# Second attention of a two-block network on TensorE: where the turned meta columns go, when the small block is turned, and a new order of work at the end of a layer

## The reference

```python
proj = h @ w_in[l]                       # 2048 x 5120
c_val, c_glu, c_gate, q, k, v, a_gate, r_x, r_gate = split(proj)
c = conv31(c_val * sigmoid(c_glu)); c = silu(layer_norm(c)); c = c @ conv_pw_w + conv_pw_b
y_conv = c * silu(c_gate)
att = window_attention(rotary(q), rotary(k), v, sinks)   # 16 heads of 64; 16 meta keys, window, sink column
y_attn = att * silu(a_gate)
r = conv4(r_x); r = rg_lru(r)            # two gates (sigmoid), exp, sqrt, scan over positions
y_lru = r * silu(r_gate)
h = layer_norm(ALPHA * h + concat(y_conv, y_attn, y_lru) @ w_out[l])
```

## Time and profile before

| | |
|---|---|
| median of 3 runs | 2809.16 us (2803.56, 2809.16, 2809.18) |
| profiled execution | 2803.59 us, its span 2801.7 us |
| TensorE products / weight loads | 2730.8 us (97%) / 2440.9 us (87%) |
| VectorE / ScalarE / GpSimd | 1828.4 us (65%) / 1416.5 us (51%) / 142.8 us (5%) |
| mean granted TensorE clock | 0.99 |

### The profile page before, as it was taken

One profiled execution on the slowest core, in us unless ns is written; L12 is line 12 of the kernel. 1 busy time (PEld: TensorE's weight loads), 2 busy tenths in 40 slices (PEclk: granted clock), 3 DMA queues, 4 the chain that ended last, 5 costly groups with the idle time before them and its releaser, 6 DMA issues.

```text
span 2801.7 us, 45189 instructions
## 1 busy us (share of the span) xinstructions
PE 2730.8 (97%) x16993; PEld 2440.9 (87%) x16993; DVE 1828.4 (65%) x2402; ACT 1416.5 (51%) x2188; POOL 142.8 (5%) x138
## 2 busy tenths in 40 slices
PE   8999999999999999999999999999999999999897
PEld 7888888888888888888888888888998899998786
DVE  7566565656565666666566656657888676788665
ACT  6444444444454544444444445445745754645764
POOL 0000000000000010101001010000000000000000
PEclk9999999999999999999999999999999999999998
DMA  6555555555555555655555555555543345543353
GB/s 212 183 180 180 180 180 179 180 178 182 180 181 187 180 166 177 186 177 180 178 179 182 177 180 180 181 185 182 171 136 121 113 157 170 163 143 117 118 173 120
DMA packets 472884, 474.43 MB, mean 169 GB/s; under 512 B 17832, under 2 KB 468032, under 8 KB 472512
## 3 DMA queue, kind: packets, MB, share of 16 engines
q1 hardware_dynamic: 472528, 472.93, 54.1%
q10 hardware_dynamic: 256, 0.11, 0.0%
HBM read 470.86 MB, written 2.13 MB: 169 GB/s over the span
## 4 chain that ended last, share of the span: by engine, by line
PE 89%; DVE 6%; ACT 4%; issue 1%; DMA 0%; SPq 0%; ACTq 0%; DVEq 0%
PE proj L1226 34%; PE proj L1228 17%; PE proj L1241 9%; PE proj L1412 5%; PE proj L1413 5%; PE proj L1414 5%; PE proj L1243 4%; PE proj L1653 2%; DVE scratch L2209 1%; DVE w_both L2040 1%; PE proj L1655 1%; PE ps_s L1313 1%; PE ps_s L1296 1%; PE ps_t L1303 1%; ACT w_both L871 1%
## 5 line engine op out<-in xcount | busy, mean ns | idle before, releaser
L1226 PE MATMUL proj<-operand,w_both 128*128 128x512 f32 x4096 | 1451.6, 399 | 5.5 <-ACT x_res L698 5.4
L1715 DVE TENSOR_TENSOR w_both<-w_raw,w_both 128x1024 fp32r<-128x1024 f32 x644 | 807.3, 1256 | 693.3 <-ACT w_both L662 692.4
L662 ACT ACTIVATE w_both<-w_raw 128x1024 fp32r<-128x1024 f32 x644 | 681.9, 1059 | 922.2 <-PE proj L1228 708.7
L1228 PE MATMUL proj<-operand,w_both 128*128 128x256 f32 x4096 | 1144.7, 279 | 0.0
L1226 PEld LDWEIGHTS proj<-operand,w_both 128*128 128x128 f32 x4096 | 769.7, 188 | 186.4 <-issue 6.2
L1228 PEld LDWEIGHTS proj<-operand,w_both 128*128 128x128 f32 x4096 | 773.1, 189 | 0.8
L1412 PE MATMUL proj<-operand,w_both 128*128 128x272 f32 (+1 forms) x1540 | 456.8, 297 | 4.5 <-DVE operand L2276 4.5
L1413 PE MATMUL proj<-operand,w_both 128*128 128x272 f32 (+1 forms) x1540 | 448.9, 292 | 0.0
L1414 PE MATMUL proj<-operand,w_both 128*128 128x272 f32 (+1 forms) x1540 | 447.9, 291 | 0.0
L2040 DVE TENSOR_TENSOR w_both<-w_raw,w_both 128x1024 fp32r<-128x1024 f32 x226 | 277.7, 1234 | 174.8 <-ACT w_both L871 173.7
L1241 PE MATMUL proj<-w_both,operand 128*128 128x512 f32 x1024 | 363.2, 399 | 0.0
(11 more groups left out here) (347 smaller groups left out, 2052.9 us busy)
## 6 DMA issues: line engine op xcount, KB each, us to landing
w_raw<-in_a_w_in_dram SPq DMA_DIRECT2D x256, 512.0 KB, 3.7
w_raw<-in_w_in_dram SPq DMA_DIRECT2D x160, 512.0 KB, 3.6
w_raw<-in_b_w_in_dram SPq DMA_DIRECT2D x128, 512.0 KB, 3.8
w_raw<-in_kv_w_dram SPq DMA_DIRECT2D x128, 512.0 KB, 3.9
w_raw<-in_a_w_out_dram SPq DMA_DIRECT2D x64, 512.0 KB, 4.5
w_raw<-in_b_w_out_dram SPq DMA_DIRECT2D x64, 512.0 KB, 3.6
w_raw<-in_w_out_dram SPq DMA_DIRECT2D x64, 512.0 KB, 3.4
scratch<-in_a_rel_bias_dram SPq DMA_DIRECT2D x16, 256.0 KB, 3.7
```

The source lines that it names most:

```text
L662: act.activation(w_hi[:, s], w_raw[:, s], ACT.Copy).then_inc(hi_ready, 1)
L1226: pe.matmul(proj[:, 2 * bank + t, :], w_hi[:, s, kk, cols], rhs[:, k, :], start=first and k == 0, stop=False)
L1228: m = pe.matmul(proj[:, 2 * bank + t, 0:S], w_lo[:, s, kk, cols], rhs[:, k, 0:S], start=False, stop=last and end)
L1715: dve.tensor_tensor(w_lo[:, s], w_raw[:, s], w_hi[:, s].bitcast(F32), ALU.subtract).then_inc(pieces_split, 1)
```

## The change

- The two turned blocks of meta columns from `s2` go to the fourth quarter of `ps_t`'s two banks, beside the other turned columns. `turn_probabilities` no longer waits for `proj_free`.
- The small block (16 x 16, from `sm`) is turned by `turn_meta_probabilities` halfway through piece 1, still into the bank of the output made before, and still behind `proj_free`. `sm` gets a second buffer (`sms`).
- `copy_turned` copies the two blocks and the other columns. A new `copy_turned_meta` copies the small block and counts `ptm_ready`. It stands behind `exponentials(i)` and one `hi`, ahead of `copy_head_outputs(i-1)`.
- The squares of the convolution go to two buffers (`conv_squares`), and both square sums follow one another.
- `TAPS_DURING` for the pairs goes from 2, 3, 4, 4, 4, 4, 1, 0 to 3, 4, 3, 3, 3, 3, 3, 0, with up to two taps ahead of the reciprocals.
- The order of ScalarE's and VectorE's work at the end of the layer is dealt anew.

```diff
 def copy_turned(i):
     act.wait_ge(turned_2, PAIRS_2 * l + i + 1)
-    bank = (o0 + U_PAIR + i) % 2
-    act.activation(ptm[0:2 * META], proj[0:2 * META, 2 * bank, 0:T], ACT.Copy).then_inc(ptm_ready, 1)
+    act.activation(ptm[0:2 * META, META:T].rearrange("p (t n) -> p t n", t=2), ps_t[0:2 * META, :, 3 * P:4 * P], ACT.Copy)
     act.activation(pt2, ps_t[:, :, 0:384], ACT.Copy).then_inc(pt2_ready, 1)
+
+def copy_turned_meta(i):
+    act.wait_ge(small_turned, PAIRS_2 * l + i + 1)
+    act.activation(ptm[0:2 * META, 0:META], proj[0:2 * META, 2 * ((o0 + U_PAIR + i) % 2), 0:META], ACT.Copy)\
+       .then_inc(ptm_ready, 1)
...
 exponentials(i)
 hi(1)
 if i >= 1:
+    copy_turned_meta(i - 1)
     copy_head_outputs(i - 1)
 divide_by_sums(i)
...
 hi(1)
 copy_turned(7)
+copy_turned_meta(7)
...
+act.wait_ge(c_centred, l + 1)
 square_conv(0)
+square_conv(1)
 hi(1)
 act.wait_ge(y_ready, 4 * l + 1)
 hi_of(att[:, 0:4, :], slice(0, 4))
-hi(1)
 copy_head_outputs(7)
-square_conv(1)
-gate_tanhs(2, a_gates[:, 4:8, :])
-hi(1)
 act.wait_ge(lru_v_ready, l + 1)
 act.activation(lru_r, lru_r, ACT.Sqrt).then_inc(lru_root, 1)
-take(U_CGATE, c_gates[:, 0:2, :], 0.5)
 hi(1)
 act.wait_ge(c_mean_ready, l + 1)
 act.activation(c_rstd, c_mean, ACT.Sqrt).then_inc(c_root_ready, 1)
+hi(1)
+take(U_CGATE, c_gates[:, 0:2, :], 0.5)
+gate_tanhs(2, a_gates[:, 4:8, :])
 gate_tanhs(3, r_gates)
 hi(1)
-act.wait_ge(y_ready_pool, l + 1)
-hi_of(att[:, 4:8, :], slice(4, 8))
 hi(1)
 act.wait_ge(c_scaled, l + 1)
...
 gate_tanhs(4, conv)
+act.wait_ge(y_ready_pool, l + 1)
+hi_of(att[:, 4:8, :], slice(4, 8))
 hi(1)
 act.wait_ge(y_ready, 4 * l + 2)
 hi_of(lru_t, slice(8, 12))
+hi(1)
 take(U_CGATE + 1, c_gates[:, 2:4, :], 0.5)
-hi(1)
 act.wait_ge(gate_used, 5 * l + 4)
 hi_of(conv, slice(12, 16))
...
 # TensorE
-    pe.wait_ge(proj_free, o0 + output + 3)
...
-    out = proj[0:2 * META, 2 * bank, :]
-    pe.transpose(out[:, 0:META], sm[0:META, 0:META, :].rearrange("p c h -> p (c h)"), ident[0:META, 0:META])
-    pe.transpose(out[:, META:144], s2[:, 0:META, :].rearrange("p c h -> p (c h)"), ident)
-    m = pe.transpose(out[:, 144:T], s2[:, 146:162, :].rearrange("p c h -> p (c h)"), ident)
+    pe.transpose(ps_t[0:2 * META, 0, 3 * P:4 * P], s2[:, 0:META, :].rearrange("p c h -> p (c h)"), ident)
+    m = pe.transpose(ps_t[0:2 * META, 1, 3 * P:4 * P], s2[:, 146:162, :].rearrange("p c h -> p (c h)"), ident)
     m.then_inc(turned_2, 1)
+
+def turn_meta_probabilities(i):
+
+    output = U_PAIR + i
+    pe.wait_ge(proj_free, o0 + output + 3)
+    pe.transpose(proj[0:2 * META, 2 * ((o0 + output) % 2), 0:META],
+                 sms[i % 2][0:META, 0:META, :].rearrange("p c h -> p (c h)"), ident[0:META, 0:META]).then_inc(small_turned, 1)
...
 turn_probabilities(i - 1)
 score(i)
-pieces(unit, norm, (1,))
+pieces(unit, norm, (1,), halfway=lambda: turn_meta_probabilities(i - 1))
 head_values(i - 1)
...
 # VectorE, layer's end
 dve.scalar_tensor_tensor(lru_r, lru_r, 1.0, lru_t, ALU.add, ALU.mult).then_inc(lru_v_ready, 1)
 lo(1)
-y_lo_of(2, att[:, 0:4, :], slice(0, 4))
-silu_of(2, a_gates[:, 4:8, :], a_gates[:, 4:8, :])
-lo(1)
 dve.wait_ge(c_sq_summed, 2 * l + 2)
 dve.tensor_scalar(c_mean, ps_s[:, 1, 0:T], 1.0 / CONV_D, LN_EPS, ALU.mult, ALU.add).then_inc(c_mean_ready, 1)
+y_lo_of(2, att[:, 0:4, :], slice(0, 4))
 dve.wait_ge(lru_root, l + 1)
 dve.wait_ge(lru_ix, l + 1)
 step(dve.tensor_tensor(lru_r, lru_r, lru_i, ALU.mult))
+lo(1)
 for t in range(CT):
     m = dve.tensor_tensor_scan(lru_t[:, t, :], lru_a[:, t, :], lru_r[:, t, :], 0.0, ALU.mult, ALU.add)
-lo(1)
 step(m)
+lo(1)
 dve.wait_ge(c_root_ready, l + 1)
 step(dve.reciprocal(c_rstd, c_rstd))
 step(refine(c_rstd, c_mean, conv_sq[:, 0, :]))
-lo(1)
 dve.tensor_tensor(conv, conv, over(c_rstd, CT), ALU.mult).then_inc(c_scaled, 1)
+silu_of(2, a_gates[:, 4:8, :], a_gates[:, 4:8, :])
+lo(1)
 silu_of(3, r_gates, r_gates)
 lo(1)
+dve.tensor_tensor(lru_t, lru_t, r_gates, ALU.mult).then_inc(y_ready, 1)
+lo(1)
+silu_of(4, conv, conv)
 y_lo_of(3, att[:, 4:8, :], slice(4, 8))
-dve.tensor_tensor(lru_t, lru_t, r_gates, ALU.mult).then_inc(y_ready, 1)
-lo(1)
-silu_of(4, conv, conv)
 lo(1)
 y_lo_of(4, lru_t, slice(8, 12))
-lo(1)
-y_lo_of(5, conv, slice(12, 16))
 ...
+lo(1)
+y_lo_of(5, conv, slice(12, 16))
```

More of the change, by code:

```diff
@@ L274, in build_program @@
         pt2 = two.take(2, 384)
-        sm = two.take(META + 1, 2)
+        sm_even = two.take(META + 1, 2)
         turn_t = two.take(2, T)
@@ L299, in build_program @@
         conv_sq = two.take(2, T)
+        sms = [sm_even, two.take(META + 1, 2)]
+        conv_squares = [conv_sq, s2.rearrange("p c h -> p (c h)")[:, 0:2 * T].rearrange("p (a b) -> p a b", a=2)]
         chunk_sum, chunk_mean, chunk_m2, chunk_off = (two.take(2, OUT_N) for _ in range(4))
@@ L1014, in divide_by_sums @@
                 def divide_by_sums(i):
+                    sm = sms[i % 2]
                     act.wait_ge(recip_2_ready, PAIRS_2 * l + i + 1)
@@ L1104, in square_conv @@
                 def square_conv(half):
[L1105 to L1108, removed]
+                    act.activation(conv_squares[half], conv[:, 2 * half:2 * half + 2, :], ACT.Square).then_inc(c_squared, 1)
                 hi(1)
                 copy_turned(7)
+                copy_turned_meta(7)
                 act.wait_ge(conv_tap, TAPS * (l + 1))
@@ L1422, in next_split, with multiply_piece @@
                 return p % PIECES
-            def multiply_piece(banks, operand_2, chunk, first, last, width=T):
+            def multiply_piece(banks, operand_2, chunk, first, last, width=T, halfway=None):
                 s = next_split()
                 for kk in range(PK):
+                    if kk == PK // 2 and halfway is not None:
+                        halfway()
                     k = chunk * PK + kk
@@ L1435, in _, with pieces @@
                 raw, norm, y = raws[l], norms[l], ys[l]
-                def pieces(output, operand_2, chunks, width=T):
+                def pieces(output, operand_2, chunks, width=T, halfway=None):
                     bank = 2 * ((o0 + output) % 2)
@@ L1442, in pieces @@
                             pe.wait_ge(proj_free, o0 + output + 1)
-                        multiply_piece(proj[:, bank:bank + 2], operand_2, chunk, chunk == 0, chunk == PIECES - 1, width)
+                        multiply_piece(proj[:, bank:bank + 2], operand_2, chunk, chunk == 0, chunk == PIECES - 1, width, halfway)
                 def mean_sums():
@@ L1628, in conv_square_sums @@
                     for t in range(2):
-                        m = pe.matmul(ps_s[:, 1, 0:T], ones, conv_sq[:, t, :], start=half + t == 0, stop=half + t == 2)
+                        m = pe.matmul(ps_s[:, 1, 0:T], ones, conv_squares[half][:, t, :], start=half + t == 0, stop=half + t == 2)
                     m.then_inc(c_sq_summed, 1)
@@ L1633, in _ @@
                 turn_probabilities(7)
-                pieces(U_CGATE, norm, (1,))
+                pieces(U_CGATE, norm, (1,), halfway=lambda: turn_meta_probabilities(7))
                 head_values(7)
                 conv_square_sums(0)
-                pieces(U_CGATE, norm, (2,))
                 conv_square_sums(1)
-                pieces(U_CGATE, norm, (3,))
+                pieces(U_CGATE, norm, (2, 3))
                 pieces(U_CGATE + 1, norm, (0, 1, 2, 3))
@@ L2251, in score_maxima @@
                     by_head = s2.rearrange("p c h -> p h c")
-                    meta_by_head = sm[0:META].rearrange("p c h -> p h c")
+                    meta_by_head = sms[i % 2][0:META].rearrange("p c h -> p h c")
                     dve.tensor_tensor(by_head[:, :, 0:144], mask_2[:, 0:144].unsqueeze(1).to_broadcast([P, 2, 144]),
@@ L2329, in _ @@
                 step(refine(c_rstd, c_mean, conv_sq[:, 0, :]))
+                dve.tensor_tensor(conv, conv, over(c_rstd, CT), ALU.mult).then_inc(c_scaled, 1)
+                silu_of(2, a_gates[:, 4:8, :], a_gates[:, 4:8, :])
                 lo(1)
-                dve.tensor_tensor(conv, conv, over(c_rstd, CT), ALU.mult).then_inc(c_scaled, 1)
                 silu_of(3, r_gates, r_gates)
                 lo(1)
-                y_lo_of(3, att[:, 4:8, :], slice(4, 8))
                 dve.tensor_tensor(lru_t, lru_t, r_gates, ALU.mult).then_inc(y_ready, 1)
@@ L2337, in _ @@
                 silu_of(4, conv, conv)
+                y_lo_of(3, att[:, 4:8, :], slice(4, 8))
                 lo(1)
                 y_lo_of(4, lru_t, slice(8, 12))
-                lo(1)
-                y_lo_of(5, conv, slice(12, 16))
                 if l + 1 < DEPTH:
```

20 lines of the change are left out of this document (12 added, 8 removed).

## The result

The changed kernel takes 2861.49 us (median of 4 runs, 2856.81 to 2862.66), the kernel before 2808.97 us on the same chip (2803.56 to 2809.18): a ratio of 1.0188, 95% interval 1.0175 to 1.0200. It is slower by 52.5 us. The profiled execution took 2856.81 us, 53.2 more than the profiled one before; its span is 2855.0 us (2801.7 before). The mean granted clock of TensorE is 0.98.

A forecast was written before the change was run, and what follows sets the result against it. TensorE, carrying 89% of the chain, was taken as the bound, losing time in pauses and at its lower clock. Attention's 39.2 and the layer ends' 9.6 gave +49 us on 2803.6 or 2809.2: forecast 2855 us, range 2828 to 2882.

The forecast's parts named there:

- The wait that comes: At head_values, waiting for the new small copy: a new pause of 3.1 us in 14 of 16 pairs.
- T+10.65: Predicted start of head_values in pair 1, 10.65 us behind the turn's start T; that pair 22.9 us.
- The clock: TensorE behind each new pause: the lower clock costs 1.6 us a pause, bounds 0 and 3.4.
- clock stays up: Rival, chance 0.12: TensorE's clock does not drop in the new pauses; 22 us less, 2833 us.
- long drop: Rival, chance 0.11: turns do not count as clock-gate work like products, so drops near 6.98 us; +25, 2880 us.
- A pair's length: Attention: a usual pair takes 21.0 us; the stretch sums to 154.3 us, +20.0 and +19.2 in the two layers.
- The layer's end: Turn 8 to pointwise product: hand-overs make TensorE wait 11.7 us for y_lo_of(3); +5.7 us, in layer 2 +3.9.
- All 15.2 us go, and with them some 6 of the clock's loss: Ahead of the turn: the 8 pauses ending with an output's take-out vanish, 15.2 us, plus some 6 us of lower clock.
- Faster: Rival, chance 0.03: the small copy comes within 5.6 us of the turn, so head_values is not late; 2795 us.

The follow-up runs named there:

- edit 1: The changed kernel with the small copy issued right behind copy_turned, ahead of the exponentials, as the only edit: 2783.42 us, ratio 0.9930.
- edit 4: The changed kernel with 25 unused products of 224 columns ahead of head_values, keeping TensorE at work in the pause: 2834.80 us, ratio 1.0116.
- edit 8: Edit 1 with the convolution taps dealt over the pairs as before the change: 2813.51 us, ratio 1.0038.
- edit 9: The kernel before with only the new dealing of the taps, the turn keeping its blocks, banks and waits: 2786.29 us, ratio 0.9927.
- edit 3: The changed kernel with the layer's end (square sums, engine orders) as before the change: 2845.05 us, ratio 1.0150.
- edit 7: The changed kernel with y_lo_of(3) moved three steps earlier on VectorE, ahead of the recurrent product: 2857.67 us, ratio 1.0194.
- edit 6: Edit 1 with another order of ScalarE's and VectorE's work at the layer's end: 2761.79 us, ratio 0.9851.
- edit 10: Edit 6 with silu_of(2) two lo later, so GpSimd's product runs beside the reciprocal, and one hi moved: 2764.23 us, ratio 0.9840.

## Why the prediction was right, and the step that was not

The forecast was 2855 us with a range of 2828 to 2882, and 2861.5 was measured; on the profiled execution 2852 against 2856.8. By its own steps:

- **The wait that comes** was the right mechanism at the right place. head_values starts 8.60 us behind its turn (8.75 predicted) in pairs 2 to 6 and waits 2.93 us (3.1). Pair 1 was predicted at T+10.65 and came at 10.55, with a pause of 4.90 us. Edit 1 shows the cause, since moving only that copy takes all 14 pauses away.
- **The clock** was sized at 1.6 us a pause; edit 4 gives 1.5 for a usual one. The trace after shows it directly: behind the pause in pair 2, some twelve products lie 0.23 us apart and the following ones 0.125, which are the two levels 1.2 and 2.4 GHz; a product of each:

```profile
2123.88 0.43 PE L1421 MATMUL proj<-operand,w_both 128*128 128x272 f32 x1
...
2126.10 0.29 PE L1421 MATMUL proj<-operand,w_both 128*128 128x272 f32 x1
```

  The rival "clock stays up" falls: all 14 pauses are followed by a stretch at 1.2 GHz (edit 4 is what it would look like, 2835 for the 2833 worked out, on a chip where the kernel before took 2803). The rival "long drop" holds for four of the 14. Length times missing clock gives 1.7 us for a usual pair (20.71 us at 0.92), but 3.3 to 3.5 for pair 1 of both layers (24.00 us at 0.86), the gates' pair of layer 1 (25.32 at 0.87) and the last pair of layer 2 (25.27 at 0.86). Its reason does not hold: no turn lies in these four low stretches (that of the first pair is over by 2104.3 us, the turns are at 2087.32 and 2111.32). Some of a low stretch lies in the pause itself, so a long one lengthens a pair by 1.0 to 1.6 us against a short one.
- **A pair's length**: 21.0 predicted, 20.71 to 20.77 measured. Pair 1 took 24.0 for 22.9, the gates' pair 25.3 and, in layer 2, 23.8 for 24.0 (no pause at the gates, as forecast), the last 24.2 and 25.3 for 23.4, in which head_values was 10.26 us behind its turn. Together 156.6 and 156.1 us for 154.3: the usual pairs were 0.25 us shorter each, and the long low stretches outweighed it.
- **The layer's end**: 49.9 and 50.0 us for 49.3 and 48.9; the pause of group 1 of the output product 12.5 and 12.7 for 11.7. Group 1 starts 41.6 us behind turn 8 for 40.8, and that has one reason. The parts up to c_scaled came some 0.4 us sooner than predicted and GpSimd's product ended 0.7 later, because it took 3.53 us beside VectorE instead of the 2.54 taken from the earlier trace rows:

```profile
2271.38 1.23 DVE L2052 TENSOR_TENSOR w_both<-w_raw,w_both 128x1024 fp32r<-128x1024 f32 x1
2271.42 3.53 POOL L653 TENSOR_TENSOR scratch<-scratch 128x1088 f32<-128x1088 f32 x1 [49.76 <-DVE scratch L2294]
...
2272.52 3.58 DVE L2294 SCALAR_TENSOR_TENSOR scratch<-scratch 128x1088 f32<-128x1088 f32 x1
...
2274.99 1.11 ACT L1042 ACTIVATE operand<-scratch 128x1088 fp32r<-128x1088 f32 x1 [1.53 <-POOL scratch L653]
...
2284.16 1.29 DVE L2288 TENSOR_TENSOR operand<-scratch,operand 128x1088 fp32r<-128x1088 f32 x1
...
2285.50 0.59 PE L1420 MATMUL proj<-operand,w_both 128*128 128x272 f32 x1 [12.52 <-DVE operand L2288]
```

  At the layer's end before nothing of VectorE ran beside that product, so the row gave its bare time. Every step behind it (att's hi_of at 2274.99, then hi, lo, the recurrent product, and so on to y_lo_of(3) at 2284.16) carries the delay on.
- **The step to correct** is "All 15.2 us go, and with them some 6 of the clock's loss". Its reading of the wait was too short: the take-out is only the last link of what held the turn. Edit 8 frees the bank and keeps VectorE's four taps a pair, and TensorE stands 18.4 us in other places (for the division, the maxima, the copies of gates and of head outputs); edit 9 keeps the bank and deals the taps evenly, and the pauses ahead of the turn fall by half with the gates' gone. So the gain in attention is mostly that of the tap dealing: 10.9 us a layer without the free bank and 15.9 with it (the table at edit 9), where within the stretch the free bank costs 2.5 us with the old taps and gives 2.5 with the new; ahead of turn 1 it gives 2.2 to 2.5 us with either. The prediction named VectorE's lateness in pairs 4 to 6, but the tap dealing, which it put under what VectorE no longer suffers from, had a price of nothing in the sum. The sum came out right because the changed kernel has both edits.
- **Faster** (2795, if head_values were not late) is close to what edit 1 is: 2783. Its sum was 12 us too high, of which 3 are the chip, where the kernel before took 2803 us and not the 2806 counted from; for the rest, one reason is that in edit 1 the clock is 1.00 all through attention and the gates' pause goes too, neither of which the 15.2 + 6 hold.

What stays open: why four of the 14 pauses were followed by the longer stretch at the lower clock (in edit 3 one more was), and why the recurrent gates' pair takes 4 us more in edit 8 than in the kernel before, with the same taps.

## What to carry to other kernels

When a wait is split in two, look up where the second half's producer stands in its engine's queue: a copy of 0.16 us behind a wait for the maxima, 2.5 us of exponentials and a hi cost 72 us over two layers, and one line moved gave it back. The instruction that a trace names as releaser is the last link only; before crediting an edit with a pause, ask what made that link late, and try each half of the edit alone. At a stage's end where three engines hand over to one another, a pause can be moved about without shrinking (edit 7); what shortened it was an order with fewer hand-overs of hi and lo behind c_scaled (edit 6, which moved several of them at once, so that the share of each is not shown). And before two spans are compared, see whether the stretch that no edit touched took as long in both.

## What the runs showed of the hardware

VectorE and GpSimd shut one another out where I had counted both at their bare times. In the rows above, a lo (two inputs) starts at 2271.38, the product of GpSimd at 2271.42; lo ends at 2272.61 after 1.23 us, and from there to the product's end at 2274.95 are 2.34 us, somewhat less than its bare 2.54. The silu that starts at 2272.52 ends at 2276.10, 1.15 behind the product, which is nearly its bare time of 1.28. So the product stood for the lo to end, and the silu for the product; by these times neither was merely slowed. Edit 6 shows it again: the second lo ends 1.1 us behind the product. In edit 10 the reciprocal, which has one input, took its usual 1.85 us beside the product and the product 2.52. The Trainium skill, "SBUF — State Buffer", Who interferes with whom, says that a VectorE instruction with two SBUF inputs and a GpSimd instruction that reads SBUF exclude one another, the first holding the port for its whole length. The three traces agree; the step behind the reciprocal in edit 10 agrees too, the small two-input product at 2237.60 taking 0.98 us where its like takes 0.44 in edit 6.
